# A two-layer MoE trunk on one core: experts placed by rank in 32-row grains, each loaded once

## The reference

```python
def _hier_moe(h, w_r1, b_r1, w_r2, b_r2, w13, w2):      # h: 1280 x 1024 in layer 0, 1024 x 1024 in layer 1
    p_grp = softmax(h @ w_r1 + b_r1); grp = argmax(p_grp); pg = p_grp[rows, grp]   # 4 groups
    logits2 = einsum('nd,gde->nge', h, w_r2) + b_r2                                # 8 experts in each
    p_in = softmax(logits2[rows, grp])
    top_p, top_j = top_k(p_in, 2); top_p = top_p / sum(top_p)
    expert = grp * 8 + top_j; wts = pg * top_p
    ...                                                  # each token goes to 2 of 32 experts
    gu = h[tok] @ w13[e]                                 # 1024 x 1024
    g, u = split(gu, 2)
    y = (silu(g) * u) @ w2[e]                            # 512 x 1024
    ...                                                  # out[token] += weight * y
```

## Time and profile before

| what | us |
|---|---|
| median of 3 runs | 3217.28 (3216.04 to 3217.42) |
| the profiled execution | 3216.31 |
| its span in the trace | 3214.7 |
| TensorE busy in the span | 2896.9 (90%) |
| first to last MoE product, layer 0 | 1223.7 to 1826.9 |
| first to last MoE product before fallback, layer 1 | 2594.5 to 3131.5 |

### The profile page before, as it was taken

The page is one execution under the profiler, slowest core; times in us unless marked ns, Lnnn a source line. Parts: engine busy times, 40 slices in busy tenths (PEclk is TensorE's granted clock), DMA queues, the critical chain, the costliest instruction groups (busy, mean ns, idle before and its releaser), DMA issues. The chain is left out here.

```text
span 3214.7 us, 34383 instructions
## 1 busy us (share of the span) xinstructions
PE 2896.9 (90%) x13041; PEld 1615.1 (50%) x13041; DVE 1299.6 (40%) x2274; ACT 792.7 (25%) x1763; POOL 689.5 (21%) x931
## 2 busy tenths in 40 slices
PE   7999998999999947999999959979999579999993
PEld 3444335888884533444444424468875334443431
DVE  4544204898882252111111154469972521111114
ACT  2211102777771100000000043146641000000001
POOL 2555201555452110010000024510001110000001
PEclk9999999999999958999999979989999789999996
DMA  6334576242413248999999574343322399999995
GB/s 252 100 102 138 199 267 176 52 98 50 99 54 128 92 188 332 412 386 415 383 413 389 216 270 135 88 124 56 67 67 93 130 410 427 426 427 427 426 417 208
DMA packets 205154, 734.36 MB, mean 228 GB/s; under 512 B 29376, under 2 KB 124784, under 8 KB 168896
## 3 DMA queue, kind: packets, MB, share of 16 engines
q1 hardware_dynamic: 104800, 633.33, 52.7%
q10 hardware_dynamic: 84896, 61.07, 5.8%
q0 software_dynamic: 15296, 37.78, 3.0%
HBM read 662.32 MB, written 87.62 MB: 233 GB/s over the span
## 5 line engine op out<-in xcount | busy, mean ns | idle before, releaser
L1707 PE MATMUL psum<-moe_ring,moe_xT 128*64 128x512 f32 (+1 forms) x2240 | 707.9, 602 | 15.6 <-DMA moe_ring<-in_e_w 13.3
L407 PE MATMUL psum<-qkv_w,act_hT 128*128 128x512 f32 x1376 | 612.0, 598 | 1.4 <-ACT act_hT L508 1.3
L1707 PEld LDWEIGHTS psum<-moe_ring,moe_xT 128*64 128x64 f32 (+1 forms) x2240 | 277.3, 162 | 410.4 <-issue 408.4
L407 PEld LDWEIGHTS psum<-qkv_w,act_hT 128*128 128x128 f32 x1376 | 256.6, 192 | 309.2 <-issue 306.9
L1728 PE MATMUL psum<-moe_ring,moe_hT 128*64 128x512 f32 (+1 forms) x1120 | 352.8, 594 | 1.6 <-DVE moe_hT L1808 1.6
L1804 DVE TENSOR_TENSOR moe_hh<-psum,moe_sg 128x512 f32<-128x512 f32 x50 | 34.6, 692 | 668.4 <-PE psum L1707 668.4
L1265 PE MATMUL psum<-wo,out_oT 128*128 128x512 f32 x576 | 255.6, 599 | 1.4 <-DVEq L1281 1.0
L1728 PEld LDWEIGHTS psum<-moe_ring,moe_hT 128*64 128x64 f32 (+1 forms) x1120 | 133.1, 160 | 184.6 <-issue 180.4
L1013 DVE TENSOR_REDUCE att_nmax<-psum 128x1 f32<-128x1280 f32 (+1 forms) x160 | 204.2, 1276 | 29.0 <-PE psum L906 28.0
L906 PE MATMUL psum<-att_kT,att_q 128*128 128x512 f32 (+1 forms) x832 | 198.0, 370 | 10.0 <-ACTq L137 5.1
L969 ACT ACTIVATE att_prob<-psum,att_nmax 128x1280 f32<-128x1280 f32 (+1 forms) x160 | 185.3, 1158 | 56.4 <-DVE att_nmax L1013 53.0
(11 more groups left out here) (252 smaller groups left out, 3301.7 us busy)
## 6 DMA issues: line engine op xcount, KB each, us to landing
moe_ring<-in_e_w SPq DMA_DIRECT2D x216, 2048.0 KB, 16.2
ada_w<-in_ada_w SPq DMA_DIRECT2D x48, 1024.0 KB, 6.5
qk_d<-qkv_stg ACTq DMA_DIRECT2D x112, 256.0 KB, 2.8
att_q<-qk_d SPq DMA_DIRECT2D x32, 640.0 KB, 12.5
att_q<-qk_d SPq DMA_DIRECT2D x64, 256.0 KB, 5.1
qkv_w<-in_a_wqkv SPq DMA_DIRECT2D x6, 2048.0 KB, 9.4
att_kT<-qk_d SPq DMA_DIRECT2D x32, 320.0 KB, 5.7
prep_y<-y_d SPq DMA_DIRECT2D x10, 1024.0 KB, 7.3
```

The lines of the kernel that those rows point to most:

```text
L407: ins = nc.tensor.matmul(psum[:, u.par, :], hT[:, k, u.t * P:(u.t + 1) * P], qw[:, u.C % 2, k], start=(k == 0), stop=(k == KD - 1))
L1707: ins = nc.tensor.matmul(psum[part, bank, :], xT[:, 4 * half + k, part], ring[:, w13[x, half] % RING, k, bank * DE:(bank + 1) * DE], start ...
```

## The change

- **Grains and rooms.** The 32 experts of a layer are ranked by their number of tokens (ties by index). The expert of rank r gets a fixed room of `ROOM[l][r]` grains of 32 rows, in a fixed order (`STREAM`). Four grains make a unit: 23 units in layer 0, 19 in layer 1, instead of 27 and 23. One expert (`OWN`, room 4: rank 7 in layer 0, rank 4 in layer 1) is taken out and done by the fallback block, which was empty.
- **Each expert is loaded once**, and its pieces stay in the ring until its last unit: 93 pieces in a layer and 3 in the fallback, instead of 105 and 3.
- **Pieces of columns.** A unit holds up to four experts. `columns` cuts each expert's stretch of the unit into aligned pieces of 128, 64 or 32 columns. In layer 0, 4 kinds of cut occur: 128 (7 units), 64+64 (3), 64 and 32 and 32 (12), 64 alone (1); in layer 1: 128 (5), 64+64 (2), 64 and 32 and 32 (6), four of 32 (5), two of 32 (1).
- **Route.** The picking is done tile by tile inside post (`dve_pick`). Ranks of experts come from comparisons and small products on TensorE, `exptab` after them. The tables are made in few large VectorE operations in bfloat16, and multiplied in bfloat16. The shares (`dve_shares`) are computed later. GpSimd's clearing of `xg` moves ahead of the barrier (`pool_route`).
- **Loads.** Only the first 4 pieces go out at `exptab`; the rest waits until the first gather has landed.
- In the fallback, w2 has its own semaphore, so that `gate_up` waits for two pieces only.

```diff
+ROOM = [[5] * 3 + [4] * 5 + [3] * 12 + [2] * 11 + [1], [8, 8, 6, 5, 4] + [3] * 5 + [2] * 10 + [1] * 12]
+STREAM = ["4323532243235322432353224323312", "1218121822315213321312263122111"]
...
+    def dve_pick(dve, l, t):
+        def first_of(val, width, code, top, one):
+            low = lowfirst[:, NE - width:NE]
+            L(V_.reduce_max(top, val, AX))
+            L(V_.scalar_tensor_tensor(code, val, top, low, ALU.is_equal, ALU.mult))
+            L(V_.reduce_max(tops[:, 3:4], code, AX))
+            L(V_.tensor_scalar(one, code, tops[:, 3:4], None, ALU.is_equal))
...
+        first_of(G, NG, ...)
+        first_of(egated[:, :], NE, ...)
+        first_of(egated[:, :], NE, ...)
+        return V_.tensor_tensor(total, pre[:, t], both[:, t], ALU.add)
...
     def sp_moe_first(sp, l):
         sp.wait_ge(s_exptab, l + 1)
-        sp_moe_loads(sp, l, 0, RING)
+        sp_moe_loads(sp, l, 0, HEAD)
     def sp_moe(sp, l):
-        sp_moe_loads(sp, l, RING, 10 ** 6)
+        sp.wait_ge(s_xg[0], xg_count(l, 0))
+        sp_moe_loads(sp, l, HEAD, 10 ** 6)
         sp_fallback(sp, l)
...
+        def columns(i):
+            for r, at, size in UNITS[l][i]:
+                while size:
+                    n = max(m for m in (1, 2, 4) if m <= size and at % m == 0)
+                    yield r, slice(GRAIN * at, GRAIN * (at + n))
+                    at, size = at + n, size - n
...
-        def gate_up(i, w13):
+        def gate_up(i):
             pe.wait_ge(s_xta, xbase + i + 1)
             pe.wait_ge(s_xtd, xbase + i + 1)
             for half in range(2):
+                arrived(i, half)
                 for k in range(4):
                     for bank in range(2):
-                        for x in range(parts):
-                            part = slice(x * rows, (x + 1) * rows)
-                            ins = nc.tensor.matmul(psum[part, bank, :], xT[:, 4 * half + k, part], ring[:, w13[x, half] % RING, k, bank * DE:(bank + 1) * DE],
+                        for r, part in columns(i):
+                            ins = nc.tensor.matmul(psum[part, bank, :], xT[:, 4 * half + k, part], ring[:, CHUNK[l][r, half] % RING, k, bank * DE:(bank + 1) * DE],
                                                    start=(half + k == 0), stop=(half == 1 and k == 3))
...
-            pe.wait_ge(s_ow, 48 * B + 48)
+            pe.wait_ge(s_ow, 32 * B + 32)
```

More of the change, by code:

```diff
@@ L39, with row_order, row_plan @@
 BIG = 1e30
[L40 to L43, removed]
+ROOM = [[5] * 3 + [4] * 5 + [3] * 12 + [2] * 11 + [1], [8, 8, 6, 5, 4] + [3] * 5 + [2] * 10 + [1] * 12]
+STREAM = ["4323532243235322432353224323312", "1218121822315213321312263122111"]
+GRAIN = 32
 NFB = 2 * NTOK // P + NE
-NBT = max(FB0) + NFB + 1
-SMALL_AT = 64 * P
+def row_order(l):
+    free = list(range(NE))
+    own = max(r for r in free if ROOM[l][r] == 4)
+    free.remove(own)
+    order = []
+    for digit in STREAM[l]:
+        r = next(r for r in free if ROOM[l][r] == int(digit))
+        free.remove(r)
+        order.append(r)
+    assert not free
+    return order, own
+def row_plan(l):
+    order, own = row_order(l)
+    units, first, at = [], [0] * NE, 0
+    for r in order:
+        first[r] = GRAIN * at
+        for b in range(at, at + ROOM[l][r]):
+            if b // 4 == len(units):
+                units.append([])
+            if not units[-1] or units[-1][-1][0] != r:
+                units[-1].append([r, b % 4, 0])
+            units[-1][-1][2] += 1
+        at += ROOM[l][r]
+    first[own] = P * len(units)
+    return units, first, own
+UNITS, FIRST, OWN = zip(*(row_plan(l) for l in range(2)))
+NU = [len(units) for units in UNITS]
+NBT = max(NU) + 1 + NFB + 1
 EMPTY = 1 << 20
@@ L1212, in build @@
     assert A.at <= KQ_AT + 8 * D * 4
+    R = Arena("route", arena0_at + 178304)
+    chosen = R("chosen", [P, 2, TA, NE])
+    both = R("both", [P, TA, NE])
+    pre = R("pre", [P, TA, NE])
+    gdist = R("gdist", [P, TA, NG])
+    gexp = R("gexp", [P, TA, NG])
+    edist = R("edist", [P, TA])
+    eexp = R("eexp", [P, TA])
+    parts_ = R("parts", [P, 3, TA])
+    tops = R("tops", [P, 4])
+    gcode = R("gcode", [P, NG])
+    gone = R("gone", [P, NG])
+    ecode = R("ecode", [P, NE])
+    egated = R("egated", [P, NE])
+    tot = R("tot", [P, NE])
+    rowmap = R("rowmap", [P, 2, P])
+    expmap = R("expmap", [P, P])
     A = Arena("postc", KQ_AT + 16 * D * 4)
@@ L1388, in build @@
-    assert A.at <= M.at, (A.at, M.at)
[L1389 to L1399, removed]
+    A = Arena("route1", M_X)
+    placed = A("placed", [P, TA, NE])
+    beyond = A("beyond", [P, TA, NE])
@@ new lines, in build @@
+    mine = A("mine", [P, 2, TA, NE])
+    slot = A("slot", [P, 2, TA])
+    sloti = A("sloti", [P, 2, 2, TA], I32)
+    blkf = A("blkf", [P, 2, TA])
+    lane = A("lane", [P, 2, TA])
+    onlane = A("onlane", [P, 2, TA, P], BF16)
+    onblk = A("onblk", [P, 2, TA, NBT], BF16)
+    value = A("value", [P, 2, TA, 2, NBT], BF16)
+    table = A("table", [P, 2, NBT])
+    assert A.at <= M.at, (A.at, M.at)
+    key = R("key", [P, NE])
+    keycol = R("keycol", [P, 1])
+    ahead = R("ahead", [P, 2, NE])
@@ L1418, in dve_route @@
[L1418 to L1429, removed]
@@ L1430, in dve_route @@
-        L(ins)
[L1431 to L1440, removed]
@@ new lines, in dve_route @@
+        V_.tensor_scalar(byrank[small], psum[small, 4, 0:NE], col(0)[small], None, ALU.is_equal).then_inc(s_rtp, 1)
+        dve.wait_ge(s_rtm, 5 * l + 3)
+        L(V_.tensor_copy(exptab[:, 0:NE], psum[:, 5, 0:NE]))
+        dve.sem_inc(s_exptab, 1)
+        dve.wait_ge(s_rtm, 5 * l + 4)
+        every = lambda row: row.unsqueeze(1).broadcast_to([P, nt, NE])
+        rank = psum[:, 0, 0:nt * NE].rearrange("p (t e) -> p t e", e=NE)
+        p3 = placed[:, 0:nt]
+        b3 = beyond[:, 0:nt]
+        L(V_.tensor_copy(fbn[:, 1], psum[:, 6, NE:2 * NE]))
@@ L1550, in pe_route, with pool_route @@
+        for q in range(2):
+            ins = nc.scalar.activation(value[:, q, 0:nt, 0], onblk[:, q, 0:nt], ACT.Copy, scale=col(1 + q))
+        ins.then_inc(s_rta, 1)
+    def pool_route(pool, l):
+        nc.gpsimd.memset(xg[:, :, :], 0.0).then_inc(s_xz, 1)
+        pool.wait_ge(s_xz, l + 1)
+        if l == 0:
+            pool.dma_start(xg[0:16, 0, 0:P], consts[0:16, 0:P]).then_inc(s_ys[0], 16)
+            pool.wait_ge(s_ys[0], 16)
     def pe_route(pe, l):
         nt = TILES[l]
-        pe.wait_ge(s_rtp, 2 * l + 1)
@@ L1553, in pe_route @@
[L1553 to L1556 removed]
+        small = slice(0, NE)
+        rank = psum[:, 0, 0:nt * NE].rearrange("p (t e) -> p t e", e=NE)
@@ new lines, in pe_route @@
+        pe.wait_ge(s_rtp, 6 * l + 1)
+        nc.tensor.matmul(psum[small, 3, 0:2], tot[:, :], ones[:, 0:2], start=True, stop=True)
+        nc.tensor.matmul(psum[:, 1, 0:NE], ones[:, :], tot[:, :], start=True, stop=True).then_inc(s_rtm, 1)
+        nc.tensor.matmul(rank, tri, both[:, 0:nt], start=True, stop=False)
+        nc.tensor.matmul(rank, ones[:, :], pre[:, 0:nt], start=False, stop=False)
+        pe.wait_ge(s_rtp, 6 * l + 2)
+        nc.tensor.matmul(psum[:, 4, 0:NE], ones[small, :], ahead[small, 0], start=True, stop=True).then_inc(s_rtm, 1)
@@ L1603, in build @@
-    PLAN = chunk_plan()
+            for i in range(NU[l] + 1):
+                new = []
+                parts = {"half0": (i, 0), "up": (i, 1), "down": (i - 1, 2)}
+                for what, (n, piece) in parts.items():
+                    if not 0 <= n < NU[l]:
+                        continue
+                    for r, at, size in UNITS[l][n]:
+                        if (r, piece) not in chunk[l]:
+                            chunk[l][r, piece] = count
+                            new.append((count, r, piece))
+                            count += 1
+                        done[chunk[l][r, piece]] = (l, n, what)
+                    steps[1] += 1
+                    ready[l, n, what] = steps[1]
+                plan.append((l, i, new))
@@ L1605, in sp_moe_loads @@
+        return plan, chunk, ready, {n: ready[at] for n, at in done.items()}, count
+    PLAN, CHUNK, READY, FREED, _ = chunk_plan()
+    CHUNKS = [3 * (NE - 1) * (l + 1) for l in range(2)]
+    assert _ == CHUNKS[1]
     def sp_moe_loads(sp, l, first, last):
@@ L1742, in pe_moe @@
         turn_x(0)
-        for pl, i, w13, w2 in PLAN:
-            if pl != l:
-                continue
+        for i in range(nu + 1):
             if i < nu:
-                gate_up(i, w13)
+                gate_up(i)
                 turn_x(i + 1)
             if i:
-                down(i - 1, w2)
+                down(i - 1)
             if i < nu:
@@ L1816, in dve_moe @@
         take_x(0)
+        dve_shares(dve, l)
         dve_fallback_table(dve, l)
@@ L1840, in fallback_slot @@
     def fallback_slot(l, part):
-        return (sum(3 * (NBIG[n] + NSMALL[n]) for n in range(l + 1)) + part) % RING
+        return (CHUNKS[l] + part) % RING
     def sp_fallback(sp, l):
@@ L1846, in sp_fallback @@
```

(6 more changed lines are left out.)

386 lines of the change are left out of this document (175 added, 211 removed).

## The result

The change takes 3493.8 us (median, 3493.6 to 3495.3) against 3216.7 before: the ratio is 1.086, with an interval of 1.084 to 1.088. The forecast was 3043. What happened is the first of the prediction's rivals, unequal strips that don't run together, and it costs more than was worked out for it (3436). "Mixed" units are those whose four grains are cut into one piece of 64 columns and two of 32.

What follows compares the result with a forecast made beforehand. TensorE was taken to bound layer 0 and the weights layer 1, each with the other just behind. From 3216.3 us, -33 - 83 - 57 - 4 + 3 = -174 gave 3042, as a median 3043, range 3010 to 3115.

Steps and rivals of the forecast that it cites:

- the first of the prediction's rivals: Mixed units of both layers: 64 and 32 strips serialize, 1.87 us instead of 0.86 per product; 3436 us, chance 0.14.
- What bounds the kernel: MoE stages: TensorE bounds layer 0 with weights just behind; weights bound layer 1 with TensorE just behind.
- Units of layer 0: Layer 0's MoE: 4 units fewer at 22.2 us, -89 us, with 6 us of waits; sum -83.
- The argument against the rival: Mixed units: the 0.15 us arises where the same columns change width; inside a mixed unit each strip keeps its own.
- Start of layer 0: Route and gather ahead of layer 0's units: first product at 1190.5 instead of 1223.7, -33 us.
- start of layer 1: Route and gather ahead of layer 1's units: first product 23 us earlier, counted inside that layer's -57.
- The new wait: Loads after the fourth piece wait for the first gather: it lands in 5 us instead of 11.5, -6 per layer.
- the walk: Unit-by-unit plan at 417 GB/s: 6 us of waits in layer 0, 80 in layer 1, whose units end at 3074.
- Fallback: Fallback block: wait for weights shrinks from 5.57 us to about 1, -4; gather and scatter of its rows, +3.
- the bounds named for the range: Whole kernel: route 9 us later per layer or 3 earlier, bandwidth -10 to +7, layer 0 balance 0 to +12; 3015 to 3085.
- the serialized case: Strips of unequal width taking turns in mixed units: +219 us, 3436, chance 0.14, left out of the range.

Runs made afterwards that it cites:

- E1: The changed kernel with each unit of 64- and 32-column pieces cut into four pieces of 32: 3064.1 us, ratio 0.952 to before.
- E4: The kernel before, with the second expert's 64 columns cut into two 32s in layer 0's 8 two-expert units: 3431.5 us in one run.
- E3: The changed kernel with products grouped by width in each half of gate_up and down, first 64 columns, then 32: 3401.1 us in one run.
- E5: The kernel before, with both experts of layer 0's 8 two-expert units cut into two 32s each, four equal pieces: 3217.9 us in one run.
- E8: E1 with four strips of 32 columns in every unit of the plan: 3062.1 us in one run.
- E2: E1 without the wait for the first gather, all 9 first pieces going out at exptab: 3064.8 us, ratio 0.953 to before.
- E6: E1 with the wait for the first gather in layer 0 only, layer 1 starting with 9 pieces: 3061.2 us, ratio 0.951 to before.
- E7: E1 with 6 first pieces in layer 1 instead of 4, still waiting for the gather: 3058.8 us, ratio 0.951 to before.

## Why the prediction was wrong, point by point

- **What bounds the kernel: right.** E1's stages show it: layer 0's units with TensorE busy 522.66 of 531.1 us, layer 1's with a DMA share of 0.96. The weights are as close behind in layer 0 (0.97) as the prediction had them:

```profile
1192.30:1723.40 531.10, 522.66 (x3252) 200.33 (x3252) 68.57 (x102) 40.87 (x69) 44.23 (x44) 0.99 0.97 402
2467.40:2978.30 510.90, 450.99 (x2862) 168.15 (x2864) 57.35 (x85) 33.64 (x57) 36.03 (x36) 0.94 0.96 400
```

- **Units of layer 0, the step that failed:** "-89 us, if strips of unequal width run together". The condition was false, and it stood under the sum of both layers: it made layer 0's units 237.7 us longer instead of 83 shorter, and layer 1's 97.7 longer instead of 34 shorter. What the earlier trace rows showed is that strips of one width run together, and the step was carried from there to mixed widths. The argument against the rival was that the price of a change shows where the same columns change width. That argument could not separate the two cases: in the earlier trace rows every change is between 128 and 64 columns, so no row had two widths on disjoint columns, and it deserved no weight. Measured, a gate_up of pieces of 64 and 32 takes 31.76 us in the change, 31.7 in E4 and 27.98 grouped by width (E3), and 13.9 in every cut of one width (E1, E5, E8). The Trainium skill's rule, that a change of tiling mode drains the engine (TensorEngine Tiling (Array Packing), section Tiling Modes), agrees with these numbers.
- **The rival's own size: too low.** It took 0.15 us for the two changes of a product from down's 7.02 against 6.87. Measured is 0.27: the other part of the price had fallen on the four transposes behind, 0.58 us (1596.54 to the next product at 1597.12) instead of 0.47, and was not counted. With 24 x 0.12 = 2.9 us more in each of 18 units, 51 us, 3436 becomes 3487; measured 3494. The rest of the rival's working, a second pass for each of 24 products, is what happened.
- **Start of layer 0:** -33 forecast, -30.5 measured; start of layer 1 -23, measured -21.1 (-23.6 in E1). `dve_pick` takes 4.2 us (1157.19 to 1161.38), VectorE's idle time in a step of post is down from 6.81 to 2.70 us at an unchanged period of 16.4, and the last step is 1.9 us longer, 1.8 forecast. Right, and nearer than the 2.5 us in between say: post's first tile stands 2.8 us later in the trace after (995.2 against 992.3), ahead of any of the steps that the sum is about.
- **The new wait:** in itself as forecast in layer 0 (5.3 us to the transposes, 5 taken), but credited with -6 in each layer. Between E1 and E2 it is worth 6.4 us in layer 0, and nothing of that is left after layer 1; E2's and E1's medians are 0.7 us apart.
- **Units, without the mix:** the walk gave 520 us for layer 0 and 503 for layer 1; E1 has 531.1 and 512.7. In layer 0 the waits are nearly as walked, 7.5 us in 4 against 6. The rest is in TensorE's work: behind its waits of 2.07 and 3.27 us the granted clock is 0.80 and 0.84 over the next 8 to 9 us, and those two gate_ups take 1.9 and 1.5 us more than their waits; and a unit with narrow pieces takes about 22.5 us where a plain one takes 22.05, with 16 such units of 23 against 8 of 27 before. In layer 1 the term that was too good is the rate: 417 GB/s taken, 400 measured in E1. There TensorE waits 59.6 us in 17 waits, less than the 80 of the walk, and works longer, 451 us against 422 (19 x 22.2), at a granted clock of 0.94 on average. Part of the lost rate is queue time that stands idle near two of the largest experts, which hold their slots over two units each: in E1's stages of 50 us the DMA share falls to 0.83 (2550 to 2600) and 0.91 (2600 to 2650). That their slots are the reason is argued, and was not tried by itself.

- **Fallback:** -1 forecast, -1.4 in E1, and that is luck: two misses cancel. The wait for weights stayed 4.63 us in E1, where 1 was forecast (-0.9 instead of -4), and its rows, taken at 3 us, cost nothing that shows.
- **Slips that change nothing:** 89 pieces at 5.5 us are 490 us, not 486, still under TensorE's 511; and the bounds named for the range give 3027 at its lower end, not 3015.
- **The chances:** 0.14 for the serialized case was too little. The whole sum hung on one behaviour that no row showed, and the price of being wrong was 400 us against a gain of 170. At near to even, the range would have had to reach 3436. The Trainium skill's rule that the prediction itself cites (TensorEngine Tiling (Array Packing), section Tiling Modes) spoke against the forecast as well.

## What to carry to other kernels

In every run here strips of TensorE's columns run side by side when they have one width, and strips of 64 and of 32 take turns: cut every product of a group to the narrowest piece that one of them needs, since four strips of 32 cost hardly more than one product of full width. When a sum rests on an operation mix that the trace doesn't show, the mix that it does show is no evidence for it; give the rival near its own weight, or change the code so that it isn't needed (here one line). And an earlier start is worth what the layer's bound makes of it: in the layer bound by its weights, no run shows that the wait that brought the first gather earlier gained anything.

## What the runs showed of the hardware

- Four weight loads of 32 columns start within one 0.16 us stretch and are hidden under the products, every 0.43 us; 128 records of 32 columns take the time of 32 of full width (13.88 and 13.74 us).
- A pair of width changes costs 0.26 to 0.27 us, whether the columns are the same (rows of before, both parts counted: 0.15 + 0.12) or disjoint (E3, after).
- A gather of 128 rows has landed 5.2 us after its issue when four pieces of 2 MB were queued ahead of it and nearly through (E1, layer 0), 7.2 us when they were less so (E1, layer 1), and 10.9 to 11.9 us behind six or nine (E2, E6, E7). It doesn't wait for all that is queued ahead: in E2 it landed at least 14 us before the last of the nine.
